# A rebuilt stretch from the first attention to the first expert, and GpSimd forming the modulation's products beside a wide pass in the first feed-forward

## The reference, cut to what matters

```
first block:   six shifts, scales and gates = silu(c) @ w_mod (1024 x 6144)
               z = norm(x) @ w_in ; attention over 256 + 256 keys ; short convolution
               x = x + gate1 * (concat(attention, conv, each normed by head) @ w_out)     # 1024 x 1024
               h = norm(x), shifted and scaled ; hierarchical routing: 4 groups of 8 experts, top 2
               x = x + gate2 * sum over chosen experts of (silu(h @ gate[e]) * (h @ up[e])) @ down[e]
               x = norm(x)                                       # 32 experts, 3 matrices of 1024 x 768 each
second block:  ada = silu(c_2) @ w_ada (1024 x 9216) + b_ada     # nine shifts, scales and gates
               x = x + 0.5 * g1 * swiglu(h, ffn1_w_in (1024 x 5632), ffn1_w_out (2816 x 1024))
               mixing: latent attention, chunk attention, gates, w_out
               x = x + 0.5 * g3 * swiglu(...) with ffn2's weights ; final norm
```

## Time and profile before

| | us |
|---|---|
| median of 3 runs | 1501.88 |
| lowest and highest run | 1498.55, 1507.09 |
| the profiled execution, and its span from first to last instruction | 1498.06, 1495.7 |
| stream of expert weights with DMA saturated | 215 to 886 |
| first feed-forward | 900 to 1091 |

### The profile page before, as it was taken

One profiled execution on the slowest core, in us unless ns is written; L12 is line 12 of the kernel. 1 busy time (PEld: TensorE's weight loads), 2 busy tenths in 40 slices (PEclk: granted clock), 3 DMA queues, 4 the chain that ended last, 5 costly groups with the idle time before them and its releaser, 6 DMA issues.

```text
span 1495.7 us, 23349 instructions
## 1 busy us (share of the span) xinstructions
PE 1445.4 (97%) x9898; PEld 1017.4 (68%) x9898; DVE 632.6 (42%) x1037; ACT 444.1 (30%) x679; POOL 27.6 (2%) x36
## 2 busy tenths in 40 slices
PE   6999999999999999999999989999999999999997
PEld 3976854444444444444344449999999778999997
DVE  5786240111100011011001019888878676655555
ACT  3434031111111111111111125344344354455453
POOL 0011000000000000000000000000020000000000
PEclk9999999999999999999999999999999999999999
DMA  9959799999999999999999995888767730455551
GB/s 359 358 210 346 288 383 426 430 432 427 428 430 431 426 430 429 427 429 431 429 427 432 429 391 206 308 310 306 247 232 281 261 113 30 155 169 199 194 168 56
DMA packets 117426, 481.00 MB, mean 322 GB/s; under 512 B 12108, under 2 KB 59465, under 8 KB 96769
## 3 DMA queue, kind: packets, MB, share of 16 engines
q1 hardware_dynamic: 115936, 476.46, 80.9%
q0 software_dynamic: 736, 2.31, 0.5%
q10 hardware_dynamic: 705, 1.51, 0.3%
HBM read 479.20 MB, written 1.06 MB: 321 GB/s over the span
## 4 chain that ended last, share of the span: by engine, by line
PE 73%; DMA 21%; DVE 2%; ACT 2%; issue 1%; SPq 0%; DVEq 0%; ACTq 0%
DMA arena<-in_w_up_dram 18%; PE psum L1584 14%; PE psum L1724 8%; PE psum L1790 7%; PE psum L1606 6%; PE psum L1702 6%; PE psum L1697 5%; PE psum L1222 3%; PE psum L1710 3%; PE psum L1692 3%; PE psum L1346 3%; PE psum L1565 2%; PE psum L1547 2%; DMA arena<-in_w_in_dram 2%; DMA arena<-in_ffn_w_in_dram 1%; PE psum L1228 1%
## 5 line engine op out<-in xcount | busy, mean ns | idle before, releaser
L1584 PE MATMUL psum<-arena,squares 128*64 128x384 f32 x2048 | 339.3, 489 | 20.6 <-DMA arena<-in_w_up_dram 11.8
L1584 PEld LDWEIGHTS psum<-arena,squares 128*64 128x64 f32 x2048 | 146.4, 137 | 215.8 <-issue 186.1
L2319 DVE TENSOR_TENSOR mixT<-mixT,psum 128x384 f32<-128x384 f32 x32 | 26.5, 828 | 496.3 <-PE psum L1584 496.3
L1606 PE MATMUL psum<-arena,small 128*64 128x512 f32 x768 | 171.9, 596 | 0.0
L1606 PEld LDWEIGHTS psum<-arena,small 128*64 128x64 f32 x768 | 52.3, 137 | 96.2 <-issue 94.4
L2386 DVE TENSOR_TENSOR ff_w_lo<-arena,ff_w_hi 128x2048 fp32r<-128x2048 f32 x44 | 100.5, 2284 | 0.0
L1702 PE MATMUL psum<-ff_x_parts,ff_w_lo 128*128 128x256 f32 x704 | 91.5, 283 | 0.0
L1702 PEld LDWEIGHTS psum<-ff_x_parts,ff_w_lo 128*128 128x128 f32 x704 | 88.9, 192 | 1.6
L1028 ACT ACTIVATE ff_w_hi<-arena 128x2048 fp32r<-128x2048 f32 x44 | 83.9, 1907 | 0.2 <-DMA arena<-in_ffn_w_in_dram 0.2
L1697 PE MATMUL psum<-ff_x_parts,ff_w_hi 128*128 128x512 f32 x336 | 79.9, 390 | 0.0
L1000 ACT ACTIVATE small<-psum 128x384 f32<-128x384 f32 x32 | 15.7, 490 | 213.6 <-PE psum L1592 213.6
(11 more groups left out here) (352 smaller groups left out, 1956.6 us busy)
## 6 DMA issues: line engine op xcount, KB each, us to landing
arena<-in_w_gate_dram SPq DMA_DIRECT2D x32, 3072.0 KB, 33.2
arena<-in_w_up_dram SPq DMA_DIRECT2D x31, 3072.0 KB, 34.8
arena<-in_w_down_dram SPq DMA_DIRECT2D x31, 3072.0 KB, 32.1
arena<-in_ffn_w_in_dram SPq DMA_DIRECT2D x44, 1024.0 KB, 7.4
arena<-in_w_ada_dram SPq DMA_DIRECT2D x18, 2048.0 KB, 12.5
arena<-in_w_mod_dram SPq DMA_DIRECT2D x11, 2048.0 KB, 15.2
arena<-in_ffn_w_out_dram SPq DMA_DIRECT2D x22, 1024.0 KB, 4.8
arena<-in_w_in_dram SPq DMA_DIRECT2D x10, 2048.0 KB, 9.4
```

Of the source, the lines that this page charges most:

```text
L1584: last = pe.matmul(b[64 * half:64 * half + 64, 0:HALF_E], lhsT=xeT[:, k, u * SLOTS:(u + 1) * SLOTS], rhs=w[:, k, half * HALF_E:(half + 1) ...
L1606: last = pe.matmul(bank[6][64 * half:64 * half + 64, :], lhsT=hiddenT[:, f % 3, 64 * (f // 3):64 * (f // 3) + 64], rhs=down[:, f, half * 5 ...
```

## The change

In the first part of the program:
- The merges become rounded products of three passes. ACT rounds the weights (`merge_round`) and the scaled mixT (`mix_hi`), DVE forms what is left (`merge_rest`, `mix_rest`).
- The four w_ada pieces move: `ada_piece` 0 before the spread, 1 inside the first merge, 2 after the last merge, 3 after the turning. Their loads are issued earlier, and gate 0 and up 0 of the first expert later.
- The norm's squares and sums go by pairs between the merges; the logits go chunk by chunk.
- Most routing operations take both token blocks in one instruction. The late columns and `ada`'s first columns are turned before the gather.
- The last expert's result is copied by DVE, not ACT.

In the first feed-forward:
- `gate_up` takes the wide pass, and ACT and DVE sum the halves, as in the second feed-forward.
- The items are formed by POOL (`mod_item`): eight products (TENSOR_SCALAR), seven of them added by a TENSOR_TENSOR. DVE keeps the turn and the sum of an item.
- The rounded weights of the two feed-forwards exchange their two slots.

```diff
+MERGES = [f"merge{i}" for i in range(4)]
+ROUNDED = {name: h + 1 for h, name in enumerate(FIRST + MERGES + SPLIT)}
...
-        ff_w_hi = {slot: rounded(f"ff_w_hi{slot}", (RING + slot // 2) * SLOT_W, SLOT_W) for slot in (0, 2)}
+        ff_w_hi = {(key, slot): rounded(f"{key}_w_hi{slot}", (RING + at) * SLOT_W, SLOT_W)
+                   for key, slot, at in (("ffn1", 2, 0), ("ffn1", 0, 1), ("ffn2", 0, 0), ("ffn2", 2, 1))}
...
+        MIX_ORDER = (4, 5, 6, 7, 0, 1, 2, 3)
+        mix_hi, mix_lo = c1_hi, c1_lo
+
+        def merge_w(i):
+
+            slot = PLACE[("pre", f"w_out{i // 2}")][0]
+            hi = (x1_lo, x1_hi)[i % 2].rearrange("p k t -> p (k t)").rearrange("p (k n) -> p k n", k=KD)
+            raw, lo = (w.rearrange("p (k n) -> p k n", k=KD)[:, :, 256 * (i % 2):256 * (i % 2) + 256]
+                       for w in (ring(slot), first_w_lo[slot]))
+            return raw, hi, lo
...
+        item_products = mixT[:, 0:4, :].rearrange("p (i a) t -> p i (a t)", i=2)
...
-            ADA_SLOTS = (3, 6, 7, 8)
+            ADA_SLOTS = (6, 3, 7, 8)
...
+            wait_item_read(sp, "z_u1")
+            load_ada_piece(0)
+            sp.wait_ge(sem("conv_done"), 1)
+            load_ada_piece(3)
+            wait_item_read(sp, readers[3])
+            load_ada_piece(1)
+            load_w_out("w_out1", "merge3")
+            sp.wait_ge(sem("attn_out"), 4)
+            load_ada_piece(2)
             for s in range(2):
                 wait_item_read(sp, readers[s])
             load_gate(0, 0)
             wait_item_read(sp, readers[2])
             load_up(0, 0)
-            load_w_out("w_out1", "merge3")
-            wait_item_read(sp, readers[3])
-            load_ada_piece(0)
-            sp.wait_ge(sem("mg_ready"), KD)
-            for i in range(1, 4):
-                load_ada_piece(i)
-            for s in (4, 5):
-                wait_item_read(sp, readers[s])
+            sp.wait_ge(sem("pieces_read"), N_PIECES + 2)
+            wait_item_read(sp, readers[4])
+            load_down(0, 0)
+            wait_item_read(sp, readers[5])
             load_gate(1, 1)
-            sp.wait_ge(sem("pieces_read"), N_PIECES + 1)
-            load_down(0, 0)
...
+            def mod_item(it, u):
+
+                w = ring(4 + u).rearrange("p (k n) -> p k n", k=KD)
+                pool.wait_ge(sem(f"ada_full{4 + u}"), it * 16 + 16)
+                for k in range(KD):
+                    if k == 0:
+                        nc.gpsimd.tensor_scalar(mod_acc[:, 0, :], w[:, 0, :], cond2[:, 0:1], 0.0, ALU.mult, ALU.add)\
+                          .then_inc(sem("mod_acc_step"), 1)
+                    else:
+                        product = item_products[:, k % 2, :]
+                        if k > 2:
+                            pool.wait_ge(sem("mod_acc_step"), it * 16 + 8 * (1 + u) + k - 1)
+                        step(nc.gpsimd.tensor_scalar(product, w[:, k, :], cond2[:, k:k + 1], 0.0, ALU.mult, ALU.add))
+                        pool.wait_ge(sem("mod_acc_step"), it * 16 + 8 * (1 + u) + k)
+                        nc.gpsimd.tensor_tensor(mod_acc[:, 0, :], mod_acc[:, 0, :], product, ALU.add)\
+                          .then_inc(sem("mod_acc_step"), 1)
+
+            for n in range(2 * FF_LOOPS):
+                if n:
+                    pool.wait_ge(sem("item_turned"), n)
+                mod_item(n // 2, n % 2)
...
+            def merge_round(i):
+
+                raw, hi, _ = merge_w(i)
+                slot, loads = PLACE[("pre", f"w_out{i // 2}")]
+                act.wait_ge(sem(f"ring_full{slot}"), 16 * loads)
+                if i >= 2:
+                    act.wait_ge(sem("job_ready"), JOB[f"merge{i - 2}"] + 1)
+                elif i == 1:
+                    act.wait_ge(sem("probs_turned"), STEPS_BEFORE["mid"])
+                nc.scalar.activation(hi, raw, ACT.Copy).then_inc(sem("mid_hi"), 1)
...
+            merge_round(1)
             act.wait_ge(sem("mg_sums"), 1)
             nc.scalar.activation(head_rstd[:, 0, :], bank[4][:, 0:32], ACT.Sqrt, bias=K("eps")).then_inc(sem("mg_root"), 1)
-            norm_squares("n2", xT, squares, "job_emptied", EMPTIED_DVE["merge0"], 1)
+            for n in range(4):
+                k = MIX_ORDER[2 * n]
+                act.wait_ge(sem("mg_ready"), 2 * n + 2)
+                nc.scalar.activation(mix_hi[:, k:k + 2, :], mixT[:, k:k + 2, :], ACT.Copy).then_inc(sem("merged_ready"), 1)
+            merge_round(2)
+            norm_squares("n2", xT, squares, "job_emptied", EMPTIED_DVE["merge0"], 1, range(1))
+            merge_round(3)
+            norm_squares("n2", xT, squares, "job_emptied", EMPTIED_DVE["merge1"], 1, range(1, 4))
...
-                    if key == "ffn1":
-                        nc.scalar.activation(gate_up_sum[:, parity, 0, :], bank[4 + 2 * parity][:, 0:T], ACT.Silu)\
-                          .then_inc(sem("ff_silu"), 1)
-                        return
                     if more:
-                        act.wait_ge(sem("ff_summed"), s - 1)
+                        act.wait_ge(sem("ff_summed"), s - 1 + past(key))
                     nc.scalar.activation(ff_b[:, :, :], psum[:, 4 + 2 * parity:6 + 2 * parity, T:2 * T], ACT.Copy)\
                       .then_inc(sem("ff_b_taken"), 1)
-                    act.wait_ge(sem("ff_summed"), s)
+                    act.wait_ge(sem("ff_summed"), s + past(key))
...
-            keep_busy(2)
             head_sums((3,), 3).then_inc(sem("mg_sums"), 1)
-            keep_busy(5)
+            pe.wait_ge(sem("cond_ready"), 5)
+
+            def ada_piece(i):
+
+                pe.wait_ge(sem(f"ada_piece_full{i}"), 16)
+                w = ring((6, 3, 7, 8)[i]).rearrange("p (k n) -> p k n", k=2)
+                for k in range(2):
+                    for m in range(4):
+                        last = pe.matmul(bank[1][32 * m:32 * m + 32, :], lhsT=cond_ada[:, 2 * i + k, :],
+                                         rhs=w[:, k, 512 * m:512 * m + 512], start=(i == 0 and k == 0), stop=(i == 3 and k == 1),
+                                         skip_group_check=True)
+                last.then_inc(sem("pieces_read"), 1)
+
+            pe.wait_ge(sem("rows_copied"), 2)
+            ada_piece(0)
...
+            def merge_job(i):
+
+                b = open_job(f"merge{i}")
+                if i >= 2:
+                    all_emptied(f"merge{i - 2}")
+                _, w_hi, w_lo = merge_w(i)
+
+                def one_pass(w, x, opens=False, closes=False, by_pair=None):
+                    for n, k in enumerate(MIX_ORDER):
+                        if opens and i == 0 and n == KD - 2:
+                            ada_piece(1)
+                        if by_pair is not None and n % 2 == 0:
+                            pe.wait_ge(sem(by_pair), n // 2 + 1)
+                        for c in range(2):
+                            last = pe.matmul(b[:, c * T:(c + 1) * T], lhsT=w[:, k, c * P:(c + 1) * P], rhs=x[:, k, :],
+                                             start=opens and n == 0 and c == 0, stop=closes and n == KD - 1, skip_group_check=True)
+                    return last
+
+                pe.wait_ge(sem("mid_hi"), ROUNDED[f"merge{i}"])
+                one_pass(w_hi, mix_hi, True, False, "merged_ready" if i == 0 else None)
+                pe.wait_ge(sem("mid_lo"), ROUNDED[f"merge{i}"])
+                one_pass(w_lo, mix_hi)
+                close_job(one_pass(w_hi, mix_lo, False, True, "merged_lo" if i == 0 else None))
...
+            merge_job(0)
+            for m in range(4):
+                last = pe.matmul(bank[0][:, 8 * m:8 * m + 8], lhsT=mod_acc[:, 0, m * P:(m + 1) * P],
+                                 rhs=block_select[:, :, :].rearrange("p i s -> p (i s)"), start=True, stop=True)
+            last.then_inc(sem("late_turned"), 1)
+            merge_job(1)
+            merge_job(2)
+            for i in range(2):
+                sums_of_pair(i)
+            merge_job(3)
+            sums_of_pair(2)
+            ada_piece(2)
+            sums_of_pair(3).then_inc(sem("norm_summed"), 1)
+            keep_busy(3)
+            spread_factor("n2", bank[7], 0)
+            keep_busy(2)
...
-                    if taken is not None and key == "ffn1":
-                        pe.wait_ge(sem("ff_act"), taken)
-                    elif taken is not None:
-                        pe.wait_ge(sem("ff_summed"), taken)
+                    if taken is not None:
+                        pe.wait_ge(sem("ff_summed"), taken + past(key))
...
-                    elif key == "ffn1":
-                        for g in range(2):
-                            for k in range(KD):
                                 pe.matmul(to[g][:, 0:T], lhsT=w_hi[:, k, g, :], rhs=ff_x_hi[:, k, :], start=(k == 0), stop=False,
...
-                def mod_steps(it, lo, hi):
-
-                    for n in range(lo, hi):
-                        u, j = n // 8, n % 8
-                        w = ring(4 + u).rearrange("p (k n) -> p k n", k=KD)
```

(16 more changed lines are left out.)

286 lines of the change are left out of this document (141 added, 145 removed).

## The result

The changed kernel takes **1548.65 us** (median of 3 runs, 1548.13 to 1554.2) against 1501.88 before: 1.0324 times, 95% interval 1.0299 to 1.035. It is 47 us slower. The prediction said 1541 us, with a range of 1492 to 1568.

A forecast was written before the change was run, and what follows sets the result against it. It took expert-weight DMA, started by the first gate pass after a gapless PE chain, and PE in the first feed-forward as bounds: 1498.1 - 4.1 + 44 = 1538, plus the median's offset 1541 us, range 1492 to 1568.

The forecast's parts named there:

- Part 1, -4.1 us: Attention to first expert: the rebuilt stretch brings the first gate pass to 205.8 from 209.94 us, the experts' end equally earlier.
- the bound of -6: Attention to first expert: the largest gain allowed, 6 us, if the handovers between engines cost nothing.
- Part 2, item of 22.2 us: First feed-forward: GpSimd's 16.7 us plus 5.5 us of blocking by VectorE per two-step item, against 17.28; +44 us in all.
- each mark that I had named: First feed-forward: turns 22 us apart, PE waiting for DVE every second step, 2.28 us remainders and POOL's instructions lengthened.
- My unheld share of each GpSimd instruction: First feed-forward: 0.34 us per scalar and 0.25 per tensor instruction leave VectorE room, so 37% of its 8.68 us hides.
- rival 2: First feed-forward: whole VectorE and GpSimd instructions exclude each other, 25.4 us an item, +73 us, 1571 us; chance 0.08.
- Item 0 has its time while expert work ends; nine items follow: First feed-forward: the first item costs nothing extra; only nine items pay 22.2 - 17.28 us each, +44.4 us.
- less 0.4 for steps outside them: First feed-forward: steps outside the nine charged items save 0.4 us, taking +44.4 to +44 us.
- Rival 1: First feed-forward: GpSimd's items fit under TensorE's two steps and add nothing, 1494 us with the offset; chance 0.30.
- the 3.8 of the median: Whole kernel: offset added because the median run is 3.8 us above the profiled execution's time.
- Rival 3: Attention to first expert gains nothing because of waits, while GpSimd's items fit in the first feed-forward; 1498 us, chance 0.05.
- The wide pass, -4.1 in the prediction's bounds: First feed-forward: PE's step falls from 8.64 to 8.44 us in 21 steps, at most 4.1 us saved.

The follow-up runs named there:

- p1_alone: Changed kernel with the first feed-forward put back (modulation products on VectorE, narrow passes), leaving only the rebuilt 140 to 215 us stretch: 1494.5 us.
- part2_alone: Kernel before, old stretch from attention to first expert kept, with only GpSimd's items and the wide pass added in the first feed-forward: 1562.73 us.
- writes_only: Changed kernel with every GpSimd instruction of an item replaced by fills of about the same length, which write SBUF and read nothing: 1495.71 us.
- products_only: Changed kernel without the seven sums of each item on GpSimd; the products are formed but not added: 1493.87 us.
- half_pool: Rebuilt stretch and narrow passes, with one of every two items on VectorE and the other on GpSimd: 1507.51 us.
- sums_one_input: Changed kernel with each of GpSimd's seven sums per item replaced by a one-input product over 1024 columns: 1544.24 us.

## Why the prediction was right, and where its sizes were off

**Part 1, -4.1 us: right in direction, too small, and by a different route.** p1_alone gained 7.4 us by medians (4.5 to 9.9) and 3.2 in its profiled span. My 4.1 lies between, but just outside the interval, and the bound of -6 does not hold the median. The steps were not right one by one. In the trace after, the chain of waits has

```profile
147.92 3.50 PE psum L1560 x16
...
175.78 1.68 PE psum L1607 x16
...
194.00 3.46 PE psum L1637 x16
...
200.09 1.23 PE psum L1287 x10
...
204.15 3.57 PE psum L1664 x32
...
208.88 7.30 PE psum L1701 x43
```

The first modulation piece took 3.50 us where I put 1.8; the norm sums ended at 186.92 (forecast 186.1) and the logits at 194.00 (192.3). VectorE's batched routing was even shorter than I had said, 3.9 us and not 4.4, so `assigned` came at 197.9 (196.7). But PE was not ready for it: the turning took 3.46 us instead of 1.78 and the piece behind it 2.63 instead of 1.8, both at a lower clock, and so positions began at 200.09. They ended at 201.32 (198.0), the gather started at 204.15 (201.4), and the first gate pass came at 208.88, not 205.8. The step that was off is the durations of PE's instructions: I took all of them from a stretch that ran at full clock. Against that one trace of before, 1.1 us of the gate pass and 2.1 of the landing were left. The rest of the measured gain probably comes from the other side: the old stretch loses the clock too in some executions (part2_alone), which the one profile of before did not show. The 25 executions of before beside p1_alone fit that: the five shortest spans (1494.8 to 1495.9 us) had a granted clock of 0.989 to 0.992, four of the five longest (1503.6 to 1504.7) 0.982 to 0.984 and the last (1506.7) 0.94. In which stretch each of them lost it was not seen.

**Part 2, item of 22.2 us: right, 22.54.** The mechanism held in each mark that I had named: turns 22 us apart, remainders and products above their own length, PE cut by waits for VectorE. Its two terms were each off, in opposite directions, so that the sum came this near is in part luck. GpSimd's chain without holds is 8 x 0.69 + 7 x 1.28 + 0.6 of gaps + 0.85 for the turn = 15.9 us, where I had 16.7 (the gaps behind a sum are about zero, I had taken 0.09 for all). The holds are the rest, 6.6 us, where I had 5.5: the groups from 932 to 1135 us give (1.61 - 0.69) x 7 + (1.33 - 1.28) x 7 = 6.8 an item, and in the item from 955 to 977 us the four products that waited, at 956.2, 959.3, 963.7 and 966.7, are 1.06, 2.29, 0.97 and 2.31 us above 0.69, 6.63 together.

```profile
L800 POOL TENSOR_SCALAR mixT<-arena,cond 128x512 f32<-128x512 f32 x63 | 101.4, 1610 | 0.0
L802 POOL TENSOR_TENSOR mod_acc<-mod_acc,mixT 128x512 f32<-128x512 f32 x63 | 83.7, 1329 | 5.3
```

So of VectorE's 8.68 us nearly a quarter hides, not 37%. What hides are the short operations of 0.42 us, which begin while a GpSimd instruction ends; the four long ones, 7.0 us, hold GpSimd for almost their full length. My unheld share of each GpSimd instruction came from one short meeting, and it does not carry over to long ones: between long ones whole instructions exclude each other, as rival 2 had it. Rival 2's 25.4 was too high because it charged the short ones too (1.7 us) and had the chain 0.8 too long. Nine items: +47.4 instead of the prediction's +44.4.

**What the sum lacked.** Two terms that I had put at nothing, about +13 us by the profiled spans:
- Ahead of the first turn. p1_alone turns its first item at 924.65, the changed kernel at 932.11, 7.5 us later. I wrote that item 0 has its time while expert work ends. It did: it was done at 925.44. But while it ran, it held VectorE. Timelines of DVE and PE:

```profile
909.01 9.10 DVE L2081 SCALAR_TENSOR_TENSOR xT<-xT,cols_a,rstd 128x256 f32<-128x256 f32 x8
...
932.11 0.70 DVE L2054 STREAM_TRANSPOSE mod_acc<-mod_acc 128x512 f32<-128x512 f32 x1
```

```profile
923.61 3.78 PE L1804 MATMUL psum<-ff_x_parts,ff_w_lo 128*128 128x256 f32 x16 [6.88 <-DVE ff_w_lo L2493]
```

The final norm's eight products took 9.10 us (3.25 in the kernel before, at 909.41), each behind one of GpSimd's instructions; the next remainder came late, and PE waited 6.88 us and then ran a pass of 1.92 us in 3.78, at half clock. The step that failed is "Item 0 has its time while expert work ends; nine items follow", with "less 0.4 for steps outside them". The delay came in each run with the rebuilt stretch in which GpSimd's items were fifteen reading instructions (first turn at 927.86 to 933.69 in five profiles) and not where it only filled (920.17) or formed products alone (923.32).
- The mixing stage, +5.4. It took 209.7 and 211.0 us in the profiles of p1_alone and before, and 212.2 to 216.7 in those with the wide pass or GpSimd's items. In the changed kernel PE starts it at a clock of 0.80 (1140 to 1160 us), after the waits of the loop. For 2.1 of the 5.4 us the rows show that: the last down products took 5.05 us (1139.73 to 1144.78, clock 0.53, 0.63 us for most pairs of matmuls) and not 2.98 as before (1088.24 to 1091.22, clock 1.00, 0.40 us a pair). The other 3.3 us are open.

By the medians part 2 cost 1548.65 - 1494.5 = 54.2 us where I had 44, and part 1 gave 7.4 where I had 4.1. The first miss, 10.2 us, is in part paid by the second, 3.3. That the sum (1498.1 - 4.1 + 44 and the 3.8 of the median, 1541.8, which I rounded down to 1541) is only some 7 us under the measured time is luck to that extent.

**The rivals.** Rival 1 (GpSimd fits, 1494) is what writes_only and products_only look like, 1495.7 and 1493.9: the figure was right for a GpSimd that does not collide, or has time left for it. Rival 3 falls with part 1's gain. The wide pass, -4.1 in the prediction's bounds, brings its 0.2 us a step (products_only), and the mixing stage was longer by as much there.

**The best version** of those run is p1_alone: the rebuilt stretch, VectorE's items and the narrow passes, 1494.5 us, 0.5% under before and 3.5% under the changed kernel.

## What to carry to other kernels

Before moving work from VectorE to GpSimd, add up what both read from SBUF: GpSimd's operations that read it and VectorE's long operations with two SBUF operands (or one at the double rate) ran one after the other here, however idle each engine looked. Here a product and its sum cost 0.75 us fused on VectorE and 0.69 + 1.28 on GpSimd, so the move raised that sum from 2 x 3.92 + 5.7 = 13.6 us an item to 8.68 + 14.5 = 23.2, of which only VectorE's shortest operations hid; GpSimd's fills (beside operations with two operands), and VectorE's reductions (0.686 us), transposes (0.712 in half_pool, as before) and operations with one operand in PSUM were free of it. A gap in a profile of one execution is not a price: look at a second execution of the old code (an experiment that leaves that code alone gives one) before reading a difference of 2 us from two traces.

## What was not expected

- The taking of turns is lopsided. In nine items GpSimd's products waited 0.92 us on average and its sums 0.05, though a sum follows its product within 0.1 us. VectorE's waiting operation got in after a sum, hardly ever after a product. Where a product of 1024 columns stood in the sum's place (sums_one_input), both waited, 0.61 and 0.34 us.
- A scaling of one operand by VectorE, 128x2048 in 1.22 us, excludes GpSimd as a subtraction of two does, for its own length.
- GpSimd filled 128x768 in 0.74 us and 128x660 in 0.65, under VectorE's subtractions, with no effect on them (2.286 and 0.426 us).
- TensorE's clock fell between 140 and 200 us in every profile but that of the kernel before, the first time with PE shown busy without a gap ahead of it (in the changed kernel PE was busy from 143 us on and the clock fell between 147 and 148; 0.78 from 145 to 150), and by different amounts for the same instructions; six more fillers there did not keep it up.
